# Gated feed-forward steps: a later turn of the inner activations, another order of the halved pieces, and one modulation sum moved

## The chip, the cores and the metric

The kernel runs on one core of a Trainium2 chip. The metric is the device time of one execution in microseconds (us); the median of three runs is quoted. A second number, the span, is the profiled execution from its first to its last instruction.

## The reference

A first block of two transformer layers (attention, a mixture of 32 experts, a small gated layer) is followed by a second block of four layers. Each layer of the second block has a dense gated feed-forward stage before and after its mixer, so that there are eight of them. The parts that matter here:

```python
def swiglu(h, w_in, w_out):
    a, b = jnp.split(h @ w_in, 2, axis=-1)
    return (jax.nn.silu(a) * b) @ w_out

mod = (c_act @ ada_w[i] + ada_b[i]).reshape(bsz, N_SUB, 3, d)
h = adaln(x, norm_g[i, 0], shift[:, 0], scale[:, 0])
x = x + MACARON_W * gate[:, 0, None] * swiglu(h, ffn_w_in[i, 0], ffn_w_out[i, 0])
```

There are 256 tokens, the model width is 1024 and the inner width 2816. The mixture of experts has the same form with 32 experts of inner width 128, each weighted by the routing.

## The kernel before

Eighteen stages follow each other. `plan_glu` lays out the two expert stages (1 and 4, `routed`) and the eight dense ones (6, 8, 9, 11, 12, 14, 15 and 17). The inner width is cut into units of 128, two units to a pair p: 11 pairs in a dense stage, 16 in an expert stage. A pair has six pieces of weights of 128x1024: four for gate and up (`gu`), each holding two of the eight blocks k of the contraction, and two for down (`down`). Each pair is worked on for two halves of 128 tokens, so that step s belongs to pair s // 2 and half s % 2. A dense stage has steps 0 to 21, an expert stage 0 to 31.

The weights are float32, and each product is made of three matmuls of halves: ACT copies a piece to its high half (`split_hi`, the rows ACT `wp<-ring`), DVE subtracts it from the raw piece to get the low half (`split_lo_v`, DVE `wp<-ring,wp`), and PE multiplies high by high, high by low and low by high. Some pieces that the next stage needs early are halved wholly or in part by POOL (`split_lo_g`). The halved pieces stand in eight slots. A slot of a gate or up piece is taken again six pieces later, so the pieces that are halved in an odd step wait for blocks k=1 and k=3 of the same step, and the two down pieces of an even step for the down products that end the step before.

In `glu_pe`, step s on PE is `gate_up(s)`: 8 blocks of 3 matmuls of 512 columns into one bank, and after that `down` for step s-2: 12 matmuls. The activations of a step go from the bank back to PE: ACT makes silu (`silu(s)`, `wk<-pb`), DVE multiplies by the other half (`up(s)`, `wk<-wk,pb`), PE turns the result in two transposes (`turn(s)`, the rows PE L280 `pb<-cst,wk`), ACT makes its high half (`high(s)`, `ex<-pb`) and DVE its low half (`low(s)`, `ex<-pb,ex`). Only then can `down` use it. `turn(s-1)` stands inside `gate_up(s)`, after the block k that is the key of the dictionary. PE works in order, so it waits there until `up(s-1)` is done. Every row of PE L273 is a matmul, whatever the product.

`glu_act` and `glu_dve` write the order of ACT and DVE out by hand: in step s first the pieces `g.split[s][:here]`, then `high(s-1)` or `low(s-1)`, then the other pieces, at s = last-1 two early pieces of the next stage, then `silu(s)` or `up(s)`. An even step has four pieces (two down, two gate and up), an odd one two. In step 0 there is no `high` and no `low`.

DVE has one more task in these stages: the modulations of later stages. `plan_ada` puts three raw chunks of `ada_w` into the stream of weights, and `ada_dve` (DVE L243, `ring<-ring,cact,prm`) makes three sums over them at the start of step s, where `g.ada[s]` is planned. Before the change this is each odd step 1 to 19 of a dense stage, up to the 96th group in all, so that stages 6 to 15 have ten groups each and stage 17 none.

SP issues all loads in the order in which chunks are planned, into a ring of 12 units of 512 KB; a load waits until the unit's former chunk was halved or summed. At pair 5 of a dense stage SP also moves a gate row: it writes it to memory, waits until it has landed, and reads it back to all partitions (`load_gate`), and the loads behind stand still for that time.

Of the kernel before, what the change touches and what calls it, by code (L numbers as in the profile page):

```python
# [338 lines left out]
def build_program(nc, stop=None):  # L339
# [398 lines left out]
    def plan_gate(st, l, s):  # L738
        gates.append((st, l, s, len(chunks)))
# [291 lines left out]
    def plan_glu(st, units, unit, order, after, routed, gate=None):  # L1031

        g = Stage()
        g.st, g.pairs, g.routed, g.gu, g.down, g.ada = st, units // 2, routed, [], [], {}
        P = g.pairs

        def made(fn, slot, by):
            c = chunk(128, UNIT, fn)
            return piece(c.dst, c, slot, by, after.get(slot) if isinstance(after, dict) else after)

        def gate_up(p, a, b, by="v"):
            for j in range(a, b):
                g.gu[p].append(made(lambda I, j=j: unit(I, p)[0][:, j * 1024:(j + 1) * 1024], order[(4 * p + j) % 6], by))
            return g.gu[p][a:b]

        def second(p, by="v"):
            at = [order[(4 * p + j) % 6 if p == P - 1 else 6 + j] for j in range(2)]
            g.down.append([made(lambda I, j=j: unit(I, p)[1][:, j * 1024:(j + 1) * 1024], at[j], by) for j in range(2)])
            return g.down[p]

        g.split = []
        g.gu.append([])
        g.first = gate_up(0, 0, 4)
        for p in range(P):
            if p + 1 < P:
                g.gu.append([])
            if gate is not None and p == P // 2:
                plan_gate(st, *gate)
            more = p + 1 < P
            late = routed and p == 2  # L1060
            by = "g" if routed and p == 1 else "v"
            a = second(p - 1, by) if p and not late else []
            b = gate_up(p + 1, 0, 2) if more else []
            g.split.append(a + b)
            if (p < 10) if not routed else (2 <= p <= 14):
                g.ada[2 * p + 1] = plan_ada()
            a = second(p - 1) if late else second(p) if not more else []
            b = gate_up(p + 1, 2, 4, "g" if routed and p == 0 else "v") if more else []
            g.split.append(a + b)
        g.order = order  # L1070
        return g
# [5 lines left out]
    def turned_at(g, s):  # L1077
        return pb[7][:, 256:512] if g.routed and s == 1 else pb[7][:, 0:256]

    def glu_pe(e, g, logits=None):  # L1080
        st, head, last = g.st, stages[g.st].head, 2 * g.pairs - 1

        def turn(*steps):
            bk.hold(e, 7, (st, "hid", steps[-1]), (x_lo, (st, "hid", steps[-1])))
            for s in steps:
                if g.routed and s < 4:
                    e.wait_ge(*v_step[st, "weighed", s])
                else:
                    e.wait_ge(*v_out[st, "glu", s])
                for j in range(2):  # L1090
                    ins = e.tp(turned_at(g, s)[:, j * 128:(j + 1) * 128], sg[s % 4][:, j * 128:(j + 1) * 128])
            ins.then_inc(*turned.up(*[(st, "hid", s) for s in steps]))

        def gate_up(s, between={}):
            p, t = divmod(s, 2)
            key = (st, "glu", s)
            ps = bk.hold(e, 4 + s % 3, key, (v_out, key))
            for k in range(KD):
                w = g.gu[p][k // 2]
                split_ready(e, w)  # L1100
                e.wait_ge(*x_lo[st, "h", t, k])
                ins = mm3_tokens(e, ps[:, :], tok_hx(k, t), [a[:, (k % 2) * 512:(k % 2 + 1) * 512] for a in (w.hi, w.lo)],
                                 k == 0, k == KD - 1)
                over = ([("used", w.at)] if t and k % 2 else []) + ([key] if k == KD - 1 else [])
                if over:
                    ins.then_inc(*product.up(*over))
                if k in between:
                    between[k]()

        def down(s, hf):  # L1110
            p, t = divmod(s, 2)
            if p == 0:
                bk.hold(e, 2 * t + hf, (st, "out", t, hf), (x_new, (st, t, hf)))
            for j, w in enumerate(g.down[p]):
                split_ready(e, w)
                e.wait_ge(*x_lo[st, "hid", s])
                ins = mm3_tokens(e, pb[2 * t + hf][:, :], [a[:, j * 128:(j + 1) * 128] for a in (eh[s % 3], el[s % 3])],
                                 [a[:, hf * 512:(hf + 1) * 512] for a in (w.hi, w.lo)], p == 0 == j,
                                 p == g.pairs - 1 and j == 1)
            over = [(st, "down", s)] if hf else []  # L1120
            over += [("used", w.at) for w in g.down[p]] if hf and t else []
            over += [(st, "out", t, hf)] if p == g.pairs - 1 else []
            if over:
                ins.then_inc(*product.up(*over))

        def whole_down(s):
            for hf in range(2):
                down(s, hf)

        second_tokens = {7: lambda: head.pe(e, 1)}  # L1130
        if g.routed:
            logits(0)
            gate_up(0, second_tokens)
            logits(1)
            for s in (1, 2, 3):
                gate_up(s)
            turn(0, 1)
            gate_up(4, {1: lambda: turn(2)})
            whole_down(0)
            whole_down(1)  # L1140
            gate_up(5, {0: lambda: turn(3), 4: lambda: turn(4)})
            whole_down(2)
            whole_down(3)
        else:
            gate_up(0, second_tokens)
            gate_up(1, {5: lambda: turn(0)})
        for s in range(6 if g.routed else 2, last):
            gate_up(s, {1: lambda: turn(s - 1)})
            whole_down(s - 2)
        gate_up(last, {1: lambda: turn(last - 1)})  # L1150
        down(last - 1, 0)
        turn(last)
        down(last - 1, 1)
        for hf in range(2):
            down(last - 2, hf)
            down(last, hf)
        boundary_pe(e, st)

    def glu_act(e, g, choice=None):
        st, last = g.st, 2 * g.pairs - 1  # L1160

        def silu(s):
            if s >= 4:
                e.wait_ge(*turned[st, "hid", s - 4])
            e.wait_ge(*product[st, "glu", s])
            e.act(sg[s % 4], bank(st, "glu", s)[:, 0:256], ACT.Silu).then_inc(*a_out.up((st, "silu", s)))

        def high(s):
            if s >= 3:
                e.wait_ge(*product[st, "down", s - 3])  # L1170
            e.wait_ge(*turned[st, "hid", s])
            e.act(eh[s % 3], turned_at(g, s), ACT.Copy).then_inc(*x_hi.up((st, "hid", s)))

        if g.routed:
            for s in range(4):
                split_hi(e, g.split[s])
                if s == 1:
                    choice()
                silu(s)
            high(0)  # L1180
            high(1)
            split_hi(e, g.split[4])
            high(2)
            silu(4)
            high(3)
            split_hi(e, g.split[5][:2])
            high(4)
            split_hi(e, g.split[5][2:])
            if g.ada.get(5) is not None:
                ada_act(e, g.ada[5])  # L1190
            silu(5)
        for s in range(6 if g.routed else 0, last + 1):
            here = 1 if s % 2 == 0 and s else 0
            split_hi(e, g.split[s][:here])
            if s:
                high(s - 1)
            split_hi(e, g.split[s][here:])
            if s == last - 1:
                split_hi(e, early(st + 1)[:2])
            if g.ada.get(s) is not None:  # L1200
                ada_act(e, g.ada[s])
            silu(s)
        boundary_act(e, st, (), [lambda: high(last)])

    def glu_dve(e, g, update, choice=None, weight=None):
# [52 lines left out]
            modulations(5)  # L1258
        for s in range(6 if g.routed else 0, last + 1):
            modulations(s)  # L1260
            here = 1 if s % 2 == 0 and s else 0
            split_lo_v(e, g.split[s][:here])
            if s:
                low(s - 1)
            split_lo_v(e, g.split[s][here:])
            if s == last - 1:
                split_lo_v(e, early(st + 1)[:2])
            up(s)
# [1918 lines left out]
```

## Time and profile before

| what | value |
|---|---|
| median of three runs | 3972.99 us (3972.85 to 3977.68) |
| the profiled execution, its own time | 3973.1 us |
| its span | 3971.3 us |
| PE busy | 3663.8 us, 92% |
| DVE busy | 2600.5 us, 65% |
| ACT busy | 1799.5 us, 45% |
| mean granted clock of TensorE | 0.956 of full |

PE, DVE, ACT, POOL and SP are the engines of the chip that do matmuls, vector work, activations, general work and the issue of loads. A busy share is a mean over all stages. The time between the span and the execution's own time is 1.8 us.

### The profile page before, as it was taken

What the parts mean: (1) busy time and instruction counts of PE and PEld (TensorE: products, weight loads), DVE (VectorE), ACT (ScalarE), POOL (GpSimd) and SP (SyncE); (2) the same over time, 40 slices, a digit from 0 to 9 for tenths busy, and PEclk for the clock granted to TensorE, in tenths of its full rate; (3) what the DMA queues carried; (4) which work ended last, traced back from release to release, by engine and by line L of the source; (5) the groups of instructions that cost most, each with busy time, mean ns of one, the idle gap of its engine ahead of it and who ended that gap; (6) DMA issues with size and microseconds to landing.
All of it is one profiled execution on the core that took longest, in us unless ns stands there. A gap on an engine that the chain in (4) does not pass through costs nothing.

```text
span 3971.3 us, 51736 instructions
## 1 busy us (share of the span) xinstructions
PE 3663.8 (92%) x19842; PEld 3010.6 (76%) x19842; DVE 2600.5 (65%) x4865; ACT 1799.5 (45%) x3151; POOL 432.4 (11%) x365
## 2 busy tenths in 40 slices
PE   7999998899899889889998989999989998989899
PEld 6767877688677767778787957878868787777677
DVE  4567765677576755567777677777567777665554
ACT  3254444544544433344546545454454544433343
POOL 2010002100000422200003420000000002322100
PEclk9899998999899989999999999999999999899999
DMA  5126752377476310068673416867338684300153
GB/s 229 54 79 247 278 198 81 122 266 278 161 270 229 115 43 1 12 217 298 216 286 136 168 55 217 290 224 281 132 133 291 223 291 154 101 28 1 59 180 106
DMA packets 181650, 670.13 MB, mean 169 GB/s; under 512 B 31264, under 2 KB 31776, under 8 KB 173216
## 3 DMA queue, kind: packets, MB, share of 16 engines
q1 hardware_dynamic: 181408, 666.83, 47.5%
q8 instruction: 160, 2.62, 0.3%
q14 instruction: 82, 0.67, 0.1%
HBM read 665.66 MB, written 1.10 MB: 168 GB/s over the span
## 4 chain that ended last, share of the span: by engine, by line
PE 79%; DVE 13%; ACT 6%; issue 2%; POOL 1%; DMA 0%; SPq 0%; DVEq 0%; ACTq 0%; POOLq 0%
PE pb L273 74%; PE pb L280 4%; DVE wp L226 3%; ACT wp L264 2%; DVE wk L238 2%; DVE wk L226 2%; DVE sq L238 1%; ACT wk L264 1%; DVE ring L243 1%; DVE hx L226 1%; ACT hx L264 1%; ACT hT L264 1%; DVE sq L226 1%; ACT sq L264 0%; POOL wp L226 0%
## 5 line engine op out<-in xcount | busy, mean ns | idle before, releaser
L273 PE MATMUL pb<-wp,hx 128*128 128x512 f32 (+1 forms) x6432 | 1605.6, 403 | 44.4 <-DVE hx L226 40.9
L226 DVE TENSOR_TENSOR wp<-ring,wp 128x1024 fp32r<-128x1024 f32 (+1 forms) x903 | 1058.3, 1206 | 608.1 <-ACT wp L264 607.4
L273 PEld LDWEIGHTS pb<-wp,hx 128*128 128x128 f32 x6432 | 1222.0, 194 | 302.4 <-DVE hx L226 24.4
L264 ACT ACTIVATE wp<-ring 128x1024 fp32r<-128x1024 f32 x936 | 958.9, 1055 | 397.7 <-PE pb L273 387.7
L273 PE MATMUL pb<-wp,ex 128*128 128x512 f32 x2928 | 702.0, 389 | 0.0
L273 PEld LDWEIGHTS pb<-wp,ex 128*128 128x128 f32 x2928 | 548.8, 188 | 113.7
L264 ACT ACTIVATE wk<-pb 128x256 f32<-128x256 f32 (+4 forms) x604 | 262.1, 439 | 612.2 <-PE pb L273 439.3
L226 POOL TENSOR_TENSOR wp<-ring,wp 128x512 fp32r<-128x512 f32 (+1 forms) x123 | 235.7, 1921 | 2693.2 <-ACT wp L264 2693.2
L273 PE MATMUL pb<-wk 128*128 128x128 f32 (+8 forms) x3008 | 389.8, 293 | 21.4 <-ACT wk L264 6.6
L273 PEld LDWEIGHTS pb<-wk 128*128 128x128 f32 (+4 forms) x3008 | 287.8, 172 | 115.6 <-issue 45.6
L273 PE MATMUL pb<-hx,wp 128*128 128x256 f32 x2688 | 344.2, 288 | 22.5 <-DVE hx L226 12.1
L273 PEld LDWEIGHTS pb<-hx,wp 128*128 128x128 f32 x2688 | 333.2, 195 | 30.8 <-issue 21.1
L243 DVE CUSTOM_DVE_ANT_0 ring<-ring,cact,prm 128x1024 f32<-128x1024 f32 x288 | 354.5, 1282 | 0.0
L264 ACT ACTIVATE ex<-pb 128x256 fp32r<-128x256 f32 x240 | 92.3, 385 | 541.9 <-PE pb L280 541.9
L280 PE MATMUL pb<-cst,wk 128*128 128x128 f32 (+2 forms) x1092 | 195.5, 282 | 52.8 <-DVE wk L226 39.7
L280 PEld LDWEIGHTS pb<-cst,wk 128*128 128x128 f32 (+2 forms) x1092 | 132.2, 141 | 112.4 <-DVE wk L226 36.4
L264 ACT ACTIVATE wk<-wk 128x256 f32<-128x256 f32 (+3 forms) x305 | 127.6, 436 | 182.4 <-DVE wk L238 65.2
L226 DVE TENSOR_TENSOR wk<-wk,pb 128x256 f32<-128x256 f32 (+1 forms) x256 | 117.7, 460 | 117.7 <-ACT wk L264 72.4
L280 PE MATMUL pb<-cst,sq 128*128 128x128 f32 x352 | 59.8, 320 | 116.7 <-DVE sq L232 109.8
L226 DVE TENSOR_TENSOR ex<-pb,ex 128x256 fp32r<-128x256 f32 x240 | 101.0, 421 | 80.7 <-ACT ex L264 79.3
L280 PEld LDWEIGHTS pb<-cst,sq 128*128 128x128 f32 x352 | 48.1, 165 | 128.4 <-issue 101.8
L226 DVE TENSOR_TENSOR wk<-pb,cst 128x256 f32<-128x256 f32 (+3 forms) x212 | 80.5, 430 | 72.2 <-PE pb L273 61.1
(176 smaller groups left out, 2748.4 us busy)
## 6 DMA issues: line engine op xcount, KB each, us to landing
ring<-weights SPq DMA_DIRECT2D x1088, 512.0 KB, 5.3
ring<-weights SPq DMA_DIRECT2D x35, 1536.0 KB, 6.5
ring<-weights SPq DMA_DIRECT2D x24, 1024.0 KB, 5.0
cst<-gate_rows SPq DMA_DIRECT2D x12, 512.0 KB, 5.1
cst<-consts SPq DMA_DIRECT2D x1, 1984.0 KB, 10.5
ring<-weights SPq DMA_DIRECT2D x1, 1280.0 KB, 5.4
ring<-weights SPq DMA_DIRECT2D x1, 1152.0 KB, 6.0
xt<-x_in SPq DMA_DIRECT2D x1, 1024.0 KB, 4.8
```

The costliest lines, as they stand in the source:

```text
L226: return self.real.tensor_tensor(out, a, b, op) if self.real else Uncounted()
L238: return self.real.scalar_tensor_tensor(out=out, in0=a, scalar=s, in1=b, op0=op0, op1=op1)
L243: return self.real.tensor_tensor_reduce(out=out, in0=a, in1=b, scale=1.0, scalar=first, op0=op0, op1=op1, accum_out=accum)
L264: return self.real.activation(out, a, func, bias=bias, scale=scale, accum_out=accum)
L273: return self.real.matmul(out, l, r, start=start, stop=stop, skip_group_check=skip)
L280: return self.real.transpose(out, a, self.identity[base:base + n, base:base + n])
```

## The change

In a dense stage, group p=0 of the modulation sums (step 1) is no longer planned; instead pair 5 has two groups, in steps 10 and 11, and the three chunks of the first of these stand ahead of the down pieces of that pair in the stream. The number of groups in a stage stays ten. `turn(s-1)` moves from behind block 1 to behind block 6 of `gate_up(s)` (for step 1 from block 5 to 6), in the dense stages from step 1 to step 20 and in the expert stages from step 6 to step 30; in the last step it stays behind block 1. In ACT and DVE, two pieces come ahead of `high(s-1)` and `low(s-1)` in each of these steps and in the last step, where there was one in even steps and none in odd ones.

```diff
@@ plan_glu
+            if p == 5 and not routed:
+                g.ada[2 * p] = plan_ada()
             a = second(p - 1, by) if p and not late else []
             b = gate_up(p + 1, 0, 2) if more else []
             g.split.append(a + b)
-            if (p < 10) if not routed else (2 <= p <= 14):
+            if (1 <= p <= 9) if not routed else (2 <= p <= 14):
                 g.ada[2 * p + 1] = plan_ada()
@@ glu_pe
-            gate_up(1, {5: lambda: turn(0)})
+            gate_up(1, {6: lambda: turn(0)})
         for s in range(6 if g.routed else 2, last):
-            gate_up(s, {1: lambda: turn(s - 1)})
+            gate_up(s, {6: lambda: turn(s - 1)})
             whole_down(s - 2)
         gate_up(last, {1: lambda: turn(last - 1)})
@@ glu_act, glu_dve
         for s in range(6 if g.routed else 0, last + 1):
-            here = 1 if s % 2 == 0 and s else 0
+            here = 2
```

## Rows read from the trace of the kernel before

**Rows 1.** The page, busy time by engine.

```profile
PE 3663.8 (92%) x19842; PEld 3010.6 (76%) x19842; DVE 2600.5 (65%) x4865; ACT 1799.5 (45%) x3151; POOL 432.4 (11%) x365
```

**Rows 2.** The chain that ended last, first steps of stage 6: start us, us, what.

```profile
1101.89 1.20 DVE ring L243
...
1105.85 2.27 DVE wp L226 x2
1108.12 0.34 DVE wk L226
...
1108.59 0.41 PE pb L280 x2
```

**Rows 3.** Timeline of PE, a step in mid-stage: start us, us, instructions.

```profile
1169.21 0.38 PE L280 MATMUL pb<-cst,wk 128*128 128x128 f32 x2
...
1173.54 2.88 PE L273 MATMUL pb<-wp,ex 128*128 128x512 f32 x12
1176.26 1.53 PE L273 MATMUL pb<-wp,hx 128*128 128x512 f32 x6
1177.62 0.38 PE L280 MATMUL pb<-cst,wk 128*128 128x128 f32 x2
```

**Rows 4.** Windows of PE, from turn(0) to turn(2) of dense stages: length, busy, granted clock.

```profile
1103.28:1118.65 15.37, 13.22 (x54) 0.89 0.95 349
1731.91:1745.66 13.75, 11.61 (x53) 1.00 1.01 337
...
2624.93:2641.46 16.53, 13.10 (x52) 0.90 0.97 340
...
3789.38:3802.45 13.07, 11.56 (x53) 1.00 0.77 252
sum 118.77, PE 100.68; mean PE 12.58
```

**Rows 5.** Timeline of PE around turn(1) of stages 6 and 12.

```profile
1103.28 0.38 PE L280 MATMUL pb<-cst,wk 128*128 128x128 f32 x2
...
1108.59 0.41 PE L280 MATMUL pb<-cst,wk 128*128 128x128 f32 x2 [2.15 <-DVE wk L226]
...
2631.57 0.66 PE L280 MATMUL pb<-cst,wk 128*128 128x128 f32 x2 [3.43 <-DVE wk L226]
```

**Rows 6.** Timeline of PE, ACT and DVE, last two steps of stages 6 and 1.

```profile
1261.76 0.38 PE L280 MATMUL pb<-cst,wk 128*128 128x128 f32 x2
...
1262.17 0.39 ACT L264 ACTIVATE ex<-pb 128x256 fp32r<-128x256 f32 x1 [0.52 <-PE pb L280]
1262.45 2.95 ACT L264 ACTIVATE wp<-ring 128x1024 fp32r<-128x1024 f32 x3
...
1270.87 2.18 ACT L264 ACTIVATE wp<-ring 128x1024 fp32r<-128x1024 f32 x2
...
1265.43 2.15 DVE L226 TENSOR_TENSOR wp<-ring,wp 128x512 fp32r<-128x512 f32 x1 [0.67 <-ACT wp L264]
...
1271.96 2.36 DVE L226 TENSOR_TENSOR wp<-ring,wp 128x1024 fp32r<-128x1024 f32 x2 [0.53 <-ACT wp L264]
...
543.49 2.67 DVE L226 TENSOR_TENSOR wp<-ring,wp 128x1024 fp32r<-128x1024 f32 x1 [0.67 <-ACT wp L264]
546.08 0.59 DVE L238 SCALAR_TENSOR_TENSOR wk<-pb,wk 128x128 f32<-128x128 f32 x2
```

**Rows 7.** Timeline of PE, last step of stage 6.

```profile
1274.50 1.53 PE L273 MATMUL pb<-wp,ex 128*128 128x512 f32 x6
```

**Rows 8.** SP's queue around the gate row of stage 6.

```profile
1152.39 0.43 SPq L283 DMA_DIRECT2D gate_rows<-mods  x1
1163.55 0.34 SPq L283 DMA_DIRECT2D cst<-gate_rows  x1
```

**Rows 9.** A window after the gate row (last: GB/s); loads, us to landing.

```profile
1168.00:1170.00 2.00, 2.00 (x12) 1.63 (x11) 2.00 (x4) 0.37 (x2) 0.00 (x0) 1.00 1.02 414
...
ring<-weights SPq DMA_DIRECT2D x1088, 512.0 KB, 5.3
```

More of the change, by code:

```diff
@@ L1260, in glu_dve @@
             modulations(s)
-            here = 1 if s % 2 == 0 and s else 0
+            here = 2
             split_lo_v(e, g.split[s][:here])
```

## The prediction

> **What bounds the kernel now.** I read the page first: PE is busy 92% of the span and DVE 65% [rows 1], so only time in which PE waits, or runs at its lower clock, can be won. Second came the timeline of a dense step in mid-stage. Its matmuls follow each other at 2.72 / 12 = 0.227 us, and from one turn to the next are 8.41 us, which is 36 matmuls (8.16) and 0.25 for the turn itself [rows 3]. PE waits for nothing there, so moving a turn wins nothing in mid-stage. Third came the chain in order of time at the start of a stage, where it leaves PE: DVE makes the three modulation sums from 1101.89 on (1.20 each), the low half of step 0 (0.34), two pieces from 1105.85 on (2.27) and up(1), and only then can PE do turn(1) at 1108.59 [rows 2]. PE has stood 2.15 us before it [rows 5]. Fourth I took the windows of PE from turn(0) to turn(2) in all eight dense stages. They hold 48 matmuls and two turns, which without a wait is 8.41 + 12 x 0.227 + 0.25 = 11.38 us; the rows say 13.07 to 16.53, and 118.77 in sum; four of the eight are shown [rows 4].
>
> **The start of a dense stage.** The loss is 118.77 - 8 x 11.38 = 27.7 us. It has two parts. Five stages (6, 9, 11, 12, 15) have a granted clock of about 0.9 in this window and three (8, 14, 17) have 1.00 [rows 4]: 15.37 us in stage 6 against 13.75 in stage 8 for the same work and the same length of wait, so 1.62 us is clock, a stretch at 1.2 instead of 2.4 GHz. With 1.6 to 1.7 in stages 6, 9, 11 and 15, whose windows agree to 0.07 us, and 5.15 - 3.43 - about 0.2 = 1.5 in stage 12, whose wait is the longest [rows 4, 5], the clock holds 8.1 us and waiting the other 19.6.
>
> The change takes the sums out of DVE's way, and turn(1) comes due later. In stage 6: DVE is free at 1101.89 and halves pieces 2 and 3 of pair 1 until 1104.2 (2.27 for two [rows 2]); ACT's halves are no later, since they wait for block 3 of step 1 at most and no longer for turn(0). Step 2 begins 6 matmuls and a turn after 1103.28 [rows 5], at 1104.9; its block 4, the first user of those pieces, is due at 1107.6, with 3.4 us to spare. turn(1) is due 21 matmuls into step 2, at 1109.7; silu(1) follows the end of step 1 at about 1105.5 and up(1) ends at about 1106.3, 3.4 us early. What is late next is the first down product, due at 24 matmuls and a turn into step 2, 1110.6: ACT makes its two pieces until about 1107.5, DVE until 1108.8. That is 1.8 us to spare, so I count no new wait, and the whole 27.7 us as won. For this I take the clock part as given back too, because the wait that goes is the only stretch without matmuls in the 10 us before the slow ones. Bounds: 19.6 if the clock stays as it is, 27.7 if it rises. Without the removal of the sums the later turn alone would leave block 4 of step 2 about 0.3 us late.
>
> The Trainium skill (TensorE: Matmul & The Clock Gate, Part 1) puts the fall of the clock down to a whole idle stretch longer than the waits at issue here. By that rule the slow matmuls would not belong to these waits, and the sum would end 8.1 us smaller. The trace is split on it: five stages slow, three not.
>
> **Mid-stage.** turn(s-1) at block 6 comes 15 matmuls (3.4 us) later. Behind it wait high, low and `down` of that step, which is at the end of the next step, 8.4 us on; hidden. In even steps silu(s) now stands behind high(s-1) and two pieces: high starts 0.41 us after the turn, the pieces 0.28 later and take 2.0, DVE follows, and up(s) ends at about 9.1 us from the step's start. turn(s) is due at 8.41 + 4.77 = 13.2. Hidden, cover 4 us. In odd steps three sums (3.6) and two pieces (2.3) on DVE end about 7 us in, and block 4 of the next step is at 11.1. Both down pieces of an even step are now halved first, sooner than before. Cost nothing.
>
> **Steps 10 and 11.** The moved group costs DVE 3.62 us in step 10. up(9) ends 1.7 us before the step, so the sums end at 1.9, the two down pieces at 4.3, and `down` needs them at 5.7; cover 1.4. Its three loads stand behind SP's gate row. SP stands 1163.55 - 1152.39 = 11.2 us between the two parts of the gate row [rows 8], and the row's issue comes 2.1 us later relative to the steps, because in odd steps the sums that free the last unit ahead of it begin after the later up. After it the loads come at 414 GB/s, 1.27 us each, and a load takes 5.3 us to land [rows 9]. So the row is done 1.9 us before step 9, the sums' chunks land up to 6.0 us into step 9 (wanted at 6.8), and the second down piece 0.2 us into step 10 (wanted at 1.2). It could be 3.8 us later before PE waits, since DVE's sums cover it. Cost nothing, by a smaller margin than now.
>
> **The end of a stage.** Here I see new waits, in all ten stages.
> First, in step 20 (30 in expert stages) the early pieces of the next stage stand between high(19) and silu(20), while turn(20) stays at block 1 of step 21, due at 8.41 + 6 x 0.227 = 9.77 from the start of step 20. The turn of 19 is at 21 matmuls, 4.77; high starts 0.41 behind it (1261.76 to 1262.17) and the pieces 0.28 behind that [rows 6], so the second is done at 7.45. DVE's part of it takes 2.15 us beside POOL, or 2.67 for a whole piece [rows 6], and up with its way to PE 0.47 (1108.12 to 1108.59 [rows 2]), with weights 0.65. That gives 10.1 in stages 6, 9 and 15 (0.33 late each), 10.8 in stages 1 and 4 (1.03), 10.6 in stage 12 (0.86), and 9.2 in stages 8, 11 and 14 where POOL has no part (a piece of 1.2, in time). Sum 3.9 us.
> Second, in the last step the two down pieces come ahead of high(20). ACT's second one waits for block 3 and ends where it does now, 1270.87 + 2.18 = 1273.05; then high takes 0.39 beside DVE's 1.22, and low(20) follows to 1274.64, at PE 1274.78 [rows 6]. The first `down` was due at 1274.50 [rows 7]: 0.28 late, in ten stages 2.8 us.
> Bounds for the end: 0 if ACT is ahead of my sums by the 0.3 to 1 us at issue, 6.7 as summed.
>
> **Sum.** 27.7 - 6.7 = 21.0 us less. The profiled execution took 3973.1 us, 1.8 more than its span, and the median of the runs is 3972.99, so both give 3952. Everything outside the ten stages stays; their starts each have a stretch at the lower clock whose length can shift with the new timing by one or two us either way.
>
> **Rivals.**
> *The clock is not given back.* The slow matmuls come from the stage's boundary and stay: 19.6 - 6.7 = 12.9 less, 3960. For it is that a wait as long as that of stage 6 left the clock of stages 8 and 14 full; against it that the slow matmuls come just behind the waits, and that those between turn(0) and the wait ran at full speed. The rule of the Trainium skill named above (TensorE: Matmul & The Clock Gate, Part 1) is for it.
> *The end costs nothing.* 27.7 less, 3945. For it is that all waits there are under 1.1 us, sums of many small terms.
> *The loads come late (slower).* In steps 9 to 12 of seven stages twelve loads instead of nine are wanted in 16.8 us, 15.2 us of transfers at the full rate, right behind 11 us without any. Beyond 3.8 us of delay each further us costs PE 7 us in all. From 3.8 + 21.0 / 7 = 6.8 us late it decides and the kernel is slower; at 8 us late it loses 4.2 x 7 = 29.4 us against the 21.0 won, which is 3981. For it is the thinner margin; against it are those 3.8 us, and that the slots of the first loads behind the gate row were freed long before.
> *Little changes.* The wait moves from turn(1) to the first down product or block 4 of step 2 with nearly the same length: within 8 us of before, about 3968. Against it are 1.8 and 3.4 us of cover.
>
> **How the numbers follow.** Forecast 0.60; clock not given back 0.16; end costs nothing 0.12; little or nothing changes, by a wait that moves or loads somewhat late, 0.07; loads late enough to be slower 0.05. The predicted time is the first's, 3952. The range goes down to 3943 (the second bound, 3945, and two us of clock at the boundaries) and up to 3963 (the clock rival and three more); above it are the 0.12 of the last two and a little. 0.2% is 8 us, about what a measurement tells from no change: faster 0.88, same 0.07, slower 0.05.
>
> **What the profile will show.** Right: windows from turn(0) to turn(2) of 11.4 us with a granted clock of 1.00 in all eight; no wait of PE for DVE `wk` in step 2; mid-stage turns 8.41 us apart; SP's gate row later in its step, no wait of ACT or DVE for a load in steps 9 to 12; PE waits of 0.3 to 1.1 us at the last two turns of the ten stages. It would be wrong by PE idle ahead of `wp,hx` or `wp,ex` matmuls in step 2 or steps 10 to 12, or by a clock below 1 in windows without a wait.

## The result: 0.7% faster, 3944.0 us

The changed kernel takes 3944.0 us (median of four runs, 3941.9 to 3952.3) against 3972.9 (3970.5 to 3977.7) for the kernel before: a ratio of 0.9932, interval 0.9917 to 0.9947. The forecast was 3952, range 3943 to 3963. The profiled execution of the changed kernel took 3952.3 us with a span of 3950.5, so profile against profile the change is worth 20.8 us, where 21.0 was forecast. All runs of the changed kernel taken together (ten) have a median of 3945.9.

The page's first line answers to [rows 1]. PE has the same 19842 matmuls in a shorter span (3663.8 us busy before); its waits for DVE `wk` at a turn have nearly halved (before: 39.7 us in 27 waits).

```profile
PE 3660.7 (93%) x19842; PEld 3007.2 (76%) x19842; DVE 2587.0 (65%) x4865; ACT 1797.9 (46%) x3151; POOL 430.2 (11%) x365
```

The waits of PE, changed kernel: what waits for what, us in total, times, longest.

```profile
PE pb L280 <- DVE wk L226: 22.0, 19, 3.7
```

The windows of PE from turn(0) to turn(2), changed kernel, the same columns as [rows 4]. turn(0) stands three matmuls later and turn(2) fifteen, so a window now holds 60 matmuls and two turns: 60 x 0.227 + 2 x 0.25 = 14.12 us without a wait.

```profile
1108.64:1122.80 14.16, 14.16 (x65) 1.00 0.79 270
1736.40:1750.57 14.17, 14.17 (x66) 1.00 0.80 263
...
2615.79:2629.89 14.10, 14.10 (x66) 1.00 0.86 300
...
3770.57:3784.68 14.11, 14.11 (x66) 1.00 0.76 255
sum 112.98, PE 112.98; mean PE 14.12
```

Busy equals length in each, the granted clock is 1.00 in all eight, and the sum is 8 x 14.12. Nothing of the 27.7 us lost there before is left: neither the waits nor the matmuls at 1.2 GHz.

The timeline of PE at the start of stage 6, changed kernel, shows why: after turn(0) come 24 matmuls and turn(1) without a gap, where [rows 5] have a wait of 2.15 us.

```profile
1102.16 6.64 PE L273 MATMUL pb<-wp,hx 128*128 128x512 f32 x21 [1.88 <-DVE hx L226]
1108.64 0.38 PE L280 MATMUL pb<-cst,wk 128*128 128x128 f32 x2
1108.78 5.74 PE L273 MATMUL pb<-wp,hx 128*128 128x512 f32 x24
1114.35 0.38 PE L280 MATMUL pb<-cst,wk 128*128 128x128 f32 x2
```

DVE in the same stretch (start, us; in brackets what it waited for) makes the low halves of the two pieces of step 1 (the first two rows), and up(1) is done at 1110.59, 3.8 us ahead of the turn that needs it at 1114.35. The last row is the two down pieces of step 2: they are done at 1113.48, 1.8 us ahead of the first `down` product at 1115.28, which is the cover that was forecast.

```profile
1106.49 1.22 DVE L226 TENSOR_TENSOR wp<-ring,wp 128x1024 fp32r<-128x1024 f32 x1
1107.87 1.23 DVE L226 TENSOR_TENSOR wp<-ring,wp 128x1024 fp32r<-128x1024 f32 x1 [0.16 <-ACT wp L264]
...
1110.17 0.42 DVE L226 TENSOR_TENSOR wk<-wk,pb 128x256 f32<-128x256 f32 x1 [0.28 <-ACT wk L264]
1111.12 2.36 DVE L226 TENSOR_TENSOR wp<-ring,wp 128x1024 fp32r<-128x1024 f32 x2 [0.53 <-ACT wp L264]
```

SP around the gate row of stage 6, changed kernel, answers to [rows 8].

```profile
1155.32 0.43 SPq L283 DMA_DIRECT2D gate_rows<-mods  x1
1166.64 0.34 SPq L283 DMA_DIRECT2D cst<-gate_rows  x1
1167.02 3.43 SPq L283 DMA_DIRECT2D ring<-weights  x6
```

Step 9 starts at 1168.5. SP is done with the row at 1166.98, 1.5 us before it, where 1.9 was forecast. In step 10, which starts at 1176.93, DVE comes to the down pieces at 1179.42, 2.5 us in (1.9 was forecast), right behind the sums, with no wait for a load. It ends them 0.8 us ahead of the `down` product at 1182.61, where 1.4 was forecast. The second of ACT's two pieces came perhaps 0.1 us late (the pair took 2.09 us, 2.01 in other steps). PE waits for nothing there. Timeline of DVE, the same kernel:

```profile
1178.22 1.28 DVE L243 CUSTOM_DVE_ANT_0 ring<-ring,cact,prm 128x1024 f32<-128x1024 f32 x1
...
1179.42 2.36 DVE L226 TENSOR_TENSOR wp<-ring,wp 128x1024 fp32r<-128x1024 f32 x2
```

The last two steps of stage 6 on PE, changed kernel, answer to [rows 6] and [rows 7].

```profile
1269.48 1.52 PE L273 MATMUL pb<-wp,hx 128*128 128x512 f32 x6
1271.08 0.41 PE L280 MATMUL pb<-cst,wk 128*128 128x128 f32 x2
1271.25 4.38 PE L273 MATMUL pb<-wp,hx 128*128 128x512 f32 x18
1275.72 1.63 PE L273 MATMUL pb<-wp,ex 128*128 128x512 f32 x6
```

turn(20) was due 6 x 0.227 = 1.36 us after 1269.48, at 1270.84, and is 0.24 late (0.33 forecast). The first `down` was due 0.27 for the turn and 18 x 0.227 after 1271.08, at 1275.44, and is 0.28 late (0.28 forecast). The rows print no wait for gaps this short; they show only against the grid of matmuls that follow each other at 0.227 us. The two longer ones have one, here stage 4 (turn(30), due 1026.42, 0.98 late; 1.03 forecast) and stage 12 (turn(20), due 2777.92, 0.78 late; 0.86 forecast):

```profile
1027.40 0.41 PE L280 MATMUL pb<-cst,wk 128*128 128x128 f32 x2 [0.81 <-DVE wk L238]
...
2778.70 0.41 PE L280 MATMUL pb<-cst,wk 128*128 128x128 f32 x2 [0.62 <-DVE wk L226]
```

### The profile page after: what moved, and what is told of

Same layout as the page of the kernel before. It is cut to its first block, busy times and chain, and to the rows that moved or that the text cites. A ratio compares the mean times of both kernels' runs of the same rounds, so it can differ in the third digit from the quotient of the medians.

```text
span 3950.5 us, 51736 instructions
## 1 busy us (share of the span) xinstructions
PE 3660.7 (93%) x19842; PEld 3007.2 (76%) x19842; DVE 2587.0 (65%) x4865; ACT 1797.9 (46%) x3151; POOL 430.2 (11%) x365
## 4 chain that ended last, share of the span: by engine, by line
PE 80%; DVE 12%; ACT 5%; issue 2%; POOL 1%; DMA 0%; SPq 0%; DVEq 0%; ACTq 0%; POOLq 0%
PE pb L273 76%; PE pb L280 5%; ACT wp L264 2%; DVE wp L226 2%; DVE wk L238 2%; DVE wk L226 2%; DVE sq L238 1%; ACT wk L264 1%; DVE hx L226 1%; DVE sq L226 1%; DVE hT L233 0%; ACT sq L264 0%; POOL wp L226 0%; DVE xt L226 0%; DMA ring<-weights 0%
```

## The experiments

Times are medians; a ratio is against the kernel before, timed in the same rounds. "Stage length" is the sum over stages of the time from the first turn to the last, by the rows of PE.

### The sums kept in step 1

The changed kernel without the edit of `plan_glu`.

```diff
-            if p == 5 and not routed:
-                g.ada[2 * p] = plan_ada()
-            if (1 <= p <= 9) if not routed else (2 <= p <= 14):
+            if (p < 10) if not routed else (2 <= p <= 14):
```

> The changed kernel with the modulation sums left in step 1 (none in step 10): the later turn and the order of the pieces alone. My theory: the turn and the order do the work. In stage 6 the sums hold DVE until about 6.3 us after it is free of the first two pieces, yet its low halves of pieces 2 and 3 are still 0.9 us ahead of blocks 4 and 6 of step 2, and up(1) is 1.2 us ahead of turn(1); so no wait, and a time within 2 us of the changed kernel (about 28 us under the one before). Rival, that the sums in the first whole step are what holds PE: a wait of 1 to 3 us comes back in step 2 of seven stages, 7 to 20 us above the changed kernel.

3951.4 us, ratio 0.9949 (0.9936 to 0.9962). The windows from turn(0) to turn(2) sum to 114.56 us, 1.6 more than in the changed kernel, with the clock at 1.00 in all eight. One stage waits, stage 12. Windows, then the timeline of PE:

```profile
2613.11:2628.53 15.42, 14.63 (x65) 1.00 0.95 359
...
2617.57 2.31 PE L273 MATMUL pb<-wp,hx 128*128 128x512 f32 x9 [0.65 <-DVE wp L226]
```

So the later turn, with the new order of the pieces, is enough by itself for nearly all of the windows' gain. The wait moves to block 4 of step 2, as the prediction said it would with the sums left in, but in one stage of eight. In stage 12 the 12 matmuls of the first `down` are also stretched, by 0.4 us, and in stage 15 by 0.2 (3.27 and 3.06 us, 2.89 without a wait). The removal of the sums, on top of the later turn, is worth 1.6 us in windows; the medians differ by more (3951.4 against 3945.9, or 3950.3 in other rounds below), which is within what the sets of runs spread.

### The sums moved alone

The kernel before with only the edit of `plan_glu`.

```diff
+            if p == 5 and not routed:
+                g.ada[2 * p] = plan_ada()
-            if (p < 10) if not routed else (2 <= p <= 14):
+            if (1 <= p <= 9) if not routed else (2 <= p <= 14):
```

> The kernel before with only the modulation sum of step 1 moved to step 10. My theory: ACT's chain (high(0) behind turn(0), two pieces, silu(1)) then holds turn(1), as in stage 17, which has no sums and waits 1.5 us. The wait shrinks from 2.2 to about 1.5 us in six stages and from 3.4 to about 2.8 in stage 12, 4 to 5 us in all, and up to 8 us more if the clock no longer falls behind the shorter wait: 3960 to 3969. Rival, the sums are the cause: nearly the whole gain of the change, 3945 to 3950.

3952.5 us, ratio 0.9952 (0.9939 to 0.9964), better than expected. PE waits at turn(1) for 1.46 to 1.50 us in all eight stages (stage 12 too, where more was expected), and the clock is 1.00 in each. Stage 12, timeline of PE, and the windows, which here hold 48 matmuls as in [rows 4]:

```profile
2616.94 0.41 PE L280 MATMUL pb<-cst,wk 128*128 128x128 f32 x2 [1.47 <-DVE wk L226]
...
2612.32:2625.41 13.09, 11.62 (x54) 1.00 0.78 255
...
sum 104.66, PE 92.82; mean PE 11.60
```

118.77 - 104.66 = 14.1 us back. What is left of the loss is 104.66 - 8 x 11.38 = 13.6 us, all of it waiting. By the waits in the rows, which sum to 18.1 us before and 11.8 here, 6.3 us of the gain are shorter waits. The other 7.8 are the clock, which came back although PE still waits. The median gained some 5 us more than the windows. By time this half of the change is worth as much as the other (3952.5 and 3951.4 us): it leaves 13.6 us of waiting at the starts, but does not pay for the ends of the stages, as the later turn does (below). The gains of the two halves overlap and do not add up.

### The end of a stage as before

The changed kernel with the end of each stage put back: turn of the last step but one at block 1, one early piece there and none in the last step.

```diff
-            gate_up(s, {6: lambda: turn(s - 1)})
+            gate_up(s, {(1 if s == last - 1 else 6): lambda: turn(s - 1)})
-            here = 2
+            here = 2 if s < last - 1 else 1 if s < last else 0
```

> The changed kernel with the last two steps of each of the ten stages as before (turn behind block 1 in the last but one step, one piece ahead of high there, none in the last). My theory: the waits at the last two turns go, 0.2 to 0.8 us at turn(20) or turn(30) in six stages and 0.28 us at the first down of the last step in ten, 6 to 7 us less than the changed kernel. Rival, the end costs nothing on the chip: within 2 us of it. Third: the time is set by stretches at the lower clock at the stages' boundaries, and moves by up to 8 us either way whatever the waits are.

3939.3 us, ratio 0.9917 (0.9903 to 0.9931). The windows of the starts sum to 113.06 (112.98 in the changed kernel), so the starts are untouched. The dense stage length is 1343.6 us against 1347.8. This beats both kernels; it was run again beside the changed one, below.

### The wait filled with matmuls

The kernel before, with 14 two-pass matmuls of 128 columns of constants ahead of turn(1) in the dense stages. Their results go to a part of a bank that nothing reads, so this is work added, none left out.

```diff
+            if steps == (1,) and not g.routed:
+                for _ in range(14):
+                    e.mm(pb[7][:, 256:384], ones[:, 0:128], ident, True, True, skip=True)
```

> The kernel before, with 14 matmuls of 128 columns of constants into an unused half of the bank just ahead of turn(1) of each dense stage, so that PE works while it waits; their results are not used. My theory, that the wait itself brings the clock down behind it: the granted clock from turn(0) to turn(2) is 1.00 in all eight stages and the time 5 to 8 us under the kernel before, while turn(1) starts when it did. Rival, the slow matmuls come from the boundary before: five stages stay at 0.89 and the time stays.

3969.5 us, ratio 0.9994 (0.9985 to 1.0003). The clock is 1.00 in all eight windows, but the added matmuls take more than the wait of 2.15 us. Timeline of PE in stage 8:

```profile
1738.56 3.29 PE L273 MATMUL pb<-cst,ones 128*128 128x128 f32 x28
1741.68 0.38 PE L280 MATMUL pb<-cst,wk 128*128 128x128 f32 x2
```

The windows sum to 117.32 us against 118.77. The clock came back, but most of it went out again: in stage 8 turn(1) starts 6.11 us behind turn(0), where it was 5.29 before, so the filler is 0.8 us too long in each of seven stages, and 1.5 in stage 17 with its shorter wait. The 5 to 8 us that were expected did not come. A second size was needed to show a time by it.

### The wait filled with fewer

The same with 9.

```diff
-                for _ in range(14):
+                for _ in range(9):
```

> As the run with 14 matmuls of constants ahead of turn(1), but with 9, about 2.0 us of work instead of 3.1, so that they fit into the wait of 2.2 us; their results are not used. My theory: turn(1) starts when it did in the kernel before, the granted clock from turn(0) to turn(2) is 1.00 in all eight stages, the eight windows sum to about 110 to 112 us instead of 118.8, and the time is 6 to 9 us under the kernel before. Rival: the matmuls of constants cost as much as they give, and the time stays within 3 us.

3958.3 us, ratio 0.9967 (0.9955 to 0.9979), 13 us faster than before (6 to 9 were expected), with 144 more matmul rows and nothing else changed. Timeline of PE and window of stage 8, and the sum of the eight windows:

```profile
1740.65 2.17 PE L273 MATMUL pb<-cst,ones 128*128 128x128 f32 x18
1742.86 0.44 PE L280 MATMUL pb<-cst,wk 128*128 128x128 f32 x2
...
1737.64:1751.36 13.72, 13.67 (x71) 1.00 1.00 335
...
sum 111.71, PE 109.72; mean PE 13.72
```

turn(1) comes no earlier than before; PE is merely kept busy until it can. The clock is 1.00 in all eight and the windows lose 118.77 - 111.71 = 7.1 us. This is the clock part of the start measured alone: 8.1 in the prediction. The median gained some 6 us more than the windows. The profile does not show where: its execution was the slowest of the six, 3969.8 us, and outside the dense stages it took 3 us more than the kernel before.

### The order of the pieces undone

The changed kernel with the old order in ACT and DVE.

```diff
-            here = 2
+            here = 1 if s % 2 == 0 and s else 0
```

> The changed kernel with the old order of ACT and DVE (one piece ahead of high and low in even steps, none in odd ones), the later turn and the moved sums kept. My theory: the order is what makes the later turn free. In an even step the second down piece is then halved behind high(s-1): high starts 5.2 us into the step, the piece is ready on PE at 7.9, and the down product wants it at 24 + 3 matmuls and a turn, 6.4. PE waits 1.5 us in each of 10 even steps of eight dense stages and 13 of two expert stages, 106 x 1.5 = 159 us: about 4100. Rival, the later turn is free in itself and the order only a matter of taste: within 5 us of the changed kernel.

4108.2 us, ratio 1.0343 (1.0326 to 1.0361), 137 us slower than before, where about 4100 us was expected. PE waits in each even step for a down piece. Timelines of PE, then ACT, in a mid-stage step of stage 6:

```profile
1184.14 0.86 PE L273 MATMUL pb<-wp,ex 128*128 128x512 f32 x3
1186.37 2.32 PE L273 MATMUL pb<-wp,ex 128*128 128x512 f32 x9 [1.38 <-DVE wp L226]
...
1183.64 0.38 ACT L264 ACTIVATE ex<-pb 128x256 fp32r<-128x256 f32 x1 [3.92 <-PE pb L280]
1183.92 2.94 ACT L264 ACTIVATE wp<-ring 128x1024 fp32r<-128x1024 f32 x3
```

ACT stands 3.92 us before high(s-1), which waits for the late turn, and three pieces are queued behind it, the second down piece among them, which could have been halved in that time. From one turn to the next are 10.08 us instead of 8.41 in every second step. The later turn is only free because the two pieces moved ahead of `high` and `low`.

### Two groups of sums in step 1

The changed kernel with two groups of modulation sums in step 1 and none in steps 10 and 19.

```diff
-            if p == 5 and not routed:
-                g.ada[2 * p] = plan_ada()
-            if (1 <= p <= 9) if not routed else (2 <= p <= 14):
+            if (p <= 8) if not routed else (2 <= p <= 14):
                 g.ada[2 * p + 1] = plan_ada()
+            if p == 0 and not routed:
+                g.more = plan_ada()
@@ glu_dve
+            if s == 1 and not g.routed and g.more is not None:
+                ada_dve(e, g.more)
```

> The changed kernel with two groups of modulation sums in step 1 and none in steps 10 and 19 of a dense stage (the same work in all). It loads DVE past the cover. My theory: DVE is free 7.2 us later, PE waits about 2.8 us ahead of block 4 of step 2 and about 0.5 us at the first down product in seven stages, 20 to 25 us, and behind those waits the clock falls in most of them (granted clock near 0.9 from turn(0) to turn(2)), up to 10 us more: 3965 to 3980. Rival for the clock: it stays at 1.00 in all stages behind waits as long as those before. Rival for the cover: no wait, 3944.

3982.0 us, ratio 1.0025 (1.0015 to 1.0036): with enough in DVE's way, the later turn gives all of its gain back, 2 us beyond the range that was expected. The wait stands ahead of block 4 of step 2: 2.61 to 2.66 us in stages 8, 9, 11 and 14, 4.21 to 4.32 in stages 6, 12 and 15. Windows of stages 8 and 15 and the sum, then the timeline of PE in the two:

```profile
1734.31:1751.73 17.42, 14.66 (x65) 1.00 0.99 372
...
3156.74:3177.55 20.81, 16.55 (x65) 0.84 0.96 353
...
sum 145.69, PE 121.77; mean PE 15.22
...
1740.78 2.33 PE L273 MATMUL pb<-wp,hx 128*128 128x512 f32 x9 [2.63 <-DVE wp L226]
...
3164.81 4.18 PE L273 MATMUL pb<-wp,hx 128*128 128x512 f32 x9 [4.26 <-DVE wp L226]
```

Nine matmuls take 2.33 us behind a wait of 2.63 and 4.18 behind one of 4.26: the second is the clock at 1.2 GHz. The longer waits come where step 1 ran at full clock (21 matmuls in 5.10 us, 6.62 elsewhere): PE arrives earlier and waits longer for the same DVE. The clock fell in these three windows (granted 0.84 to 0.92) and not in the other four, so of the expectation that it falls in most, three of seven came true, and its rival holds for four.

### The last step alone put back

The changed kernel with only the order of the last step as before.

```diff
-            here = 2
+            here = 2 if s < last else 0
```

> The changed kernel with no piece ahead of high and low in the very last step of each stage, as before; the last but one step stays changed. My theory: the wait of 0.28 us at the first down product of the last step goes in ten stages, the wait at turn(20) or turn(30) stays (0.2 to 0.8 us in six stages): from turn(0) to the last turn a dense stage takes 0.28 us less than in the changed kernel (168.2 in stage 17, so 167.9; 169.0 in stage 12, so 168.7), 2.8 us in all. Rival: the piece for the down product is then late instead, and nothing is won.

One run, 3939.5 us beside 3967.4 for the kernel before. The dense stage length is 1345.1 us, 2.7 less than the changed kernel's 1347.8 (8 x 0.28 = 2.2 was forecast). From turn(20) to turn(21) are 5.69 to 5.76 us where the changed kernel has 6.05 to 6.10, so each stage gains about 0.35; turn(30) of the expert stages still waits 0.80 and 0.81 us and stage 12's turn(20) 0.61. The two causes at the end are separate, and each has nearly the size that was worked out.

### The changed kernel and the better end, side by side

Both again in the same rounds. The first is the changed kernel itself, the second the one with the end as before.

> The changed kernel once more, for a comparison with the next one on the same chip. My theory: 3944, 26 to 29 us under the kernel before. Rival: its profiled execution (3952) was the typical one.

> The changed kernel with the last two steps of each stage as before, once more, on the same chip as the changed kernel. My theory: 5 to 7 us under the changed kernel. Rival: the two agree within 2 us, since the clock at the boundaries sets the difference.

Changed: 3950.3 us, ratio 0.9943 (0.9928 to 0.9958), 20.8 us under the kernel before in the same rounds (3971.1), so less than the 26 to 29 expected, and nearer to the rival. End as before: 3935.9 us (3933.6 to 3942.1), ratio 0.9914 (0.9902 to 0.9927). The intervals don't meet, and the medians differ by 14.4 us, where 5 to 7 were expected. Stage 6's end in each, timeline of PE; first the changed kernel:

```profile
1262.36 1.52 PE L273 MATMUL pb<-wp,hx 128*128 128x512 f32 x6
1263.96 0.41 PE L280 MATMUL pb<-cst,wk 128*128 128x128 f32 x2
1264.13 4.36 PE L273 MATMUL pb<-wp,hx 128*128 128x512 f32 x18
1268.60 1.63 PE L273 MATMUL pb<-wp,ex 128*128 128x512 f32 x6
```

and with the end as before, where every step stands on the grid of 0.227 us:

```profile
1259.48 1.53 PE L273 MATMUL pb<-wp,hx 128*128 128x512 f32 x6
1260.85 0.38 PE L280 MATMUL pb<-cst,wk 128*128 128x128 f32 x2
1260.99 4.36 PE L273 MATMUL pb<-wp,hx 128*128 128x512 f32 x18
1265.18 1.53 PE L273 MATMUL pb<-wp,ex 128*128 128x512 f32 x6
```

From the turn of step 20 to the first `down` of the last step are 4.64 us in the first and 4.33 in the second. Dense stage length 1348.1 against 1343.5, expert 488.8 against 486.4: the end costs 4.6 + 2.4 = 7.0 us, where 6.7 was forecast; the spans of these two profiles differ by 10.3, and the other 3.3 lie outside the stages. Over all runs of the two (ten and eleven) the medians differ by 8.6 us.

### The kernel before, once more

No edit: a second profile of the kernel before.

> The kernel before, unchanged, for a second profile. My theory: the waits at turn(1) are the same to 0.1 us (2.2 us in six stages, 3.4 in one, 1.5 in the last), but the stages in which the clock falls behind them are others, four to seven of those seven. Rival: the same five stages fall, so that the fall belongs to the program and not to chance.

3969.4 us. The waits at turn(1) are those of the first profile, 2.16 to 2.23 us in five stages, but 3.44 in stages 9 and 12 (3.43 in stage 12 alone in the first), and 1.49 in stage 17. Windows of stages 8 and 9, the same columns as [rows 4], and the sum:

```profile
1727.62:1742.99 15.37, 13.18 (x53) 0.89 0.93 343
1924.86:1941.36 16.50, 13.06 (x53) 0.90 0.94 343
...
sum 121.36, PE 102.07; mean PE 12.76
```

Stage 8, at full clock in the first profile, now ran at 0.89 behind the same wait, and took 15.37 us, exactly what stage 6 took there. So whether the clock falls behind a wait of 2.2 us differs between executions of one program, and its price, 15.37 - 13.75 = 1.62 us, does not.

The rows show what goes with the fall. Windows of PE from 1.8 to 1.3 us before turn(0) (length, busy, granted clock), stages 6 and 8 of the first profile, then stage 8 of the second:

```profile
1101.48:1101.98 0.50, 0.50 (x3) 0.50 0.65 98
1730.11:1730.61 0.50, 0.50 (x4) 1.00 0.67 123
...
1725.82:1726.32 0.50, 0.50 (x3) 0.50 0.81 180
```

Ahead of each of the eight waits of about 2.2 us with a fall behind them, the clock was still at 1.2 GHz in this half microsecond (0.50); ahead of the three without one it was already at 2.4 (1.00). So the fall goes with the moment at which the clock rose in step 1, which differs between executions. No run moved that moment by itself, and the waits of 1.5 us kept the clock with either.

## Why the prediction was right

**The start of a stage (27.7 forecast).** Right in mechanism and size. The windows of the changed kernel hold no wait and no slow matmul. (The prediction named 11.4 us as their length and forgot that turn(0) and turn(2) move too; with 12 more matmuls the same windows are 14.12.) By stage length, the dense stages before take 1376.2 us, of which 8 x 0.68 = 5.4 are only the earlier place of turn(0); 1370.8 - 1343.5 (the starts changed, the ends as before) = 27.3 us.

**Its clock part (8.1 forecast).** Right, and shown apart from the wait: filling the wait gave 7.1 us back in the windows (9.7 against the second profile of the kernel before), and nothing else was touched. The rival that the clock is not given back (3960) is out. The rule it leaned on, of the Trainium skill (TensorE: Matmul & The Clock Gate, Part 1), that the clock falls after a whole idle stretch, by which it would have stayed up behind waits like these, does not hold in this case: of the 11 waits of 2.15 to 2.25 us in the two profiles of the kernel before, 8 have a granted clock of 0.89 in their window, and the 24 windows of the two kernels with filled waits and of the changed kernel have 1.00. Here the measurement decides.

**What is late next.** Right that nothing is, with both edits. The prediction said that without the removal of the sums block 4 of step 2 would be 0.3 us late; measured, a wait of 0.65 us in stage 12 and none there in the others. It was argued from stage 6, and there the step was mis-sized: it counts both pieces against block 4, which needs only the first. With the sums kept, DVE had the low half of that one at about 1108.2, 1.7 us ahead of block 4 at 1109.9. The rival that the wait only moves was a real danger and not a far one: two groups of sums in step 1 bring it about in seven stages, 32 us above the changed kernel in the same rounds (3950.3).

**Mid-stage at nothing.** Right: turns stay 8.41 us apart (1131.21, 1139.63, 1148.04 in stage 6; in some stages every second step takes 8.45, in both kernels). But the prediction did not price the order of the pieces by itself. It is the cover for the later turn, and without it the kernel takes 158 us more than the changed kernel in the same rounds.

**Steps 10 and 11 at nothing.** Right, with less cover left than forecast (DVE at its down pieces 2.5 us into the step, 1.9 forecast; 0.8 us to spare, 1.4 forecast). The rival that the loads come late is out.

**The ends (6.7 forecast).** Right term by term: 0.24, 0.78 and 0.98 us for turn(20) and turn(30) where 0.33, 0.86 and 1.03 stood, 0.28 for the first `down` where 0.28 stood, and 7.0 in all by the two kernels side by side. The first terms sum to 3.5 us; the other 3.5 are the 0.35 us that each last step is longer. The rival that the end costs nothing is out, though its time, 3945, is the one nearest the median.

**The sum, and what it missed.** 27.3 - 7.0 = 20.3 us, and the spans of the two first profiles differ by 20.8. By parts, the dense stages gave 1370.8 - 1347.8 = 23.0 us (forecast 23.6: the 27.7 less 4.1 at their ends), the expert stages lost 3.5 (2.6), and everything else gave 1.2 (nothing). In the second profile of the changed kernel the same parts are 22.7 gained, 0.7 lost and 4.9 gained, and the spans differ by 26.9, so that the agreement of the total to 0.2 us was luck, and that of the dense stages was not.

The medians differ by 28.9 us in the first rounds, by 20.8 in the later ones, and by 26 over all runs; the interval of the first ratio, 0.9917 to 0.9947, is 21 to 33 us. So the excess over the forecast is at the edge of what was measured, and absent in the later rounds. If it is real, the mis-sized term is the last of the prediction, that outside the ten stages one or two us could shift either way. Those stretches hold the same instructions in every kernel run here, yet in the profiles of before, changed, changed again and the two with the end as before they take 2107.0, 2105.8, 2102.1, 2098.7 and 2093.1 us. The mean granted clock goes with them: 0.956, 0.958, 0.960, 0.961 and 0.962. But the second profile of the kernel before has 2102.4, at 0.957, so one and the same kernel differs by 4 to 6 us there between two profiles. Over all thirteen profiles, the five with the early turn take 2101.0 to 2109.4 us, 2105.7 in the mean, and the eight with the late turn 2093.1 to 2105.8, 2099.3 in the mean. That the fewer waits leave PE more often at full clock at the stages' boundaries would fit this, and so would chance between executions, since one kernel's own runs spread over 21 us (the changed kernel's, 3935.4 to 3956.5). No run here tells these apart, and it stays open whether, and why, some 5 us more than the stages account for were won.

## What to carry to other kernels

When a consumer moves later in an in-order engine, move the producers queued behind the old hand-over in the same edit, and check the first and the last steps of the loop by themselves: here the steady state gave nothing and cost nothing, the starts held 27 us and the ends cost 7. A short wait on PE has two prices, its length and the clock behind it; a wait of 1.5 us in place of 2.2, or useless matmuls in the gap, got the second back where the first stayed. And when a change wins, put back each part that has no gain of its own: doing so at the ends gave the best version, 3936 to 3939 us.

## What the runs showed of the hardware

- Waits of PE on their way into a dense stage, by length, and how many had matmuls at 1.2 GHz in the window behind them: 1.5 us, 0 of 10; 2.15 to 2.25 us, 8 of 11; 2.6 us, 0 of 4; 3.4 to 4.3 us, 6 of 6. Length alone does not decide, as the 2.6 us waits show. Of the 11 in the middle, all 8 with a fall had a granted clock of 0.50 from 1.8 to 1.3 us before turn(0), the 3 without one had 1.00. With the gap filled by matmuls, 0 of 16.
- A fall behind a wait of 2.2 us costs 1.6 to 1.7 us here, in every stage and in both profiles; behind the longest waits it was an estimated 1.5 (stage 12 of the kernel before) and 1.8 us (20.81 - 17.42 less 1.63 of longer wait, two sums in step 1).
- A matmul of 128 columns of float32 constants, in its two passes, took 2.17 / 9 = 0.24 us in the filler of 9 and 3.29 / 14 = 0.235 in that of 14.
- Executions of one kernel spread over up to 0.5% (21 us). Between profiles of kernels that share the stretches outside the ten stages, those stretches differed by 14 us among the five named above, and the mean granted clock with them; between two profiles of one kernel by 4 to 6 us.
